# Joining a normalisation to a recurrence, and rotation tables to a projection, in a two-block model kernel

## The chip, the cores and the metric

The kernel runs on one core of a Trainium2 chip, as one program. The metric is the time of one execution on the device, in microseconds (us); of several executions the median counts. All arrays are float32. TensorE multiplies matrices, VectorE (DVE), ScalarE (ACT) and GpSimd (POOL) do elementwise work, and SyncE (SP) issues loads and stores.

## The reference

Two transformer-like blocks are computed over one sequence of 1024 tokens of width 1024. The parts that matter here are these.

In the first block eight heads of 64 run a recurrence over the tokens (`rwkv7_scan`). Its output y is normalised for each token and head, scaled and shifted for each channel, a bonus is added, and the sum is multiplied by a gate:

```python
y = rwkv7_scan(r_h, heads(decay), k_h, v_h, -kk, kk * a_h)
y = head_layernorm(y, LNX_EPS).reshape(Bn, T, C_R) * lnx_w + lnx_b   # mean and variance over the 64 of a head
bonus = jnp.sum(r_h * k_h * r_k, axis=-1, keepdims=True) * v_h
return ((y + bonus.reshape(Bn, T, C_R)) * g).astype(p.dtype)
```

In the second block eight attention heads have 128 plain and 64 rotated dimensions. The rotated part of the key, `k_pe`, is one of the outputs of the block's input projection and is shared by all heads:

```python
q = rmsnorm_2(q, qk_q_g)
k = rmsnorm_2(k, qk_k_g)                      # k = [k_nope, k_pe], mean of squares over 192
ang = positions.astype(jnp.float32)[..., None] * inv_freq
cos, sin = jnp.cos(ang)[:, :, None, :], jnp.sin(ang)[:, :, None, :]
q = concat(q[..., :128], apply_rope(q[..., 128:], cos, sin)); k = concat(k[..., :128], apply_rope(k[..., 128:], cos, sin))
```

## The kernel before

The program is a row of seventeen stages. Each is a block with a hand-written instruction order for every engine and semaphores between them. At the end of a stage its semaphores are cleared and all engines meet at a barrier. Stages hand their results on through scratch tensors in HBM. All tensors are laid out with channels on the 128 partitions and tokens along the free axis.

The order around the change is: `norm_dense_stage` "in1" (first input projection), `mlstm_stage`, `rwkv_scan_stage`, `rwkv_finish_stage`, the dense stages out1, up and down, `norm_stage`, `norm_dense_stage` "in2" (second input projection), the dense stages uq and ukv, `attention_stage`, and five more.

**The recurrence** (`rwkv_scan_stage`) handles 8 blocks b of 128 tokens, each of two chunks c of 64. It keeps three blocks of inputs loaded (`load(b)` on SP: `ar`, `bt`, `kt`, `vt`). For each block TensorE makes the products of the chunks (`first_products`), five groups of turned or multiplied inputs (`misc`), and a triangular inverse in five levels (`step_t`, `step_x`). Woven into the levels of block b are the three serial parts of block b-1 for each chunk: `z_part`, `u_part` and `s_part`. The last makes the change of the state, in PSUM bank `BANK_S`, and completes y, in `BANK_Y`. ScalarE copies PSUM to SBUF (`misc_copy`, `t_copy`, `z_copy`, `u_copy`, `y_copy`), VectorE masks the products (`first_masks`), merges levels (`level`) and updates the state (`state`), and GpSimd sets X and XT to the identity and masks two products. y of a block goes to HBM. After the loop the serial parts of the last block follow alone.

**The normalisation** (`rwkv_finish_stage`) is a stage of its own over four tiles of 128 channels by 1024 tokens: it loads y, the bonus and the gate, takes means and variances with matmuls, and ends with four VectorE passes for each tile. Its output goes to `cat`, which the dense stage out1 loads.

**The second input projection** runs over 37 tiles i of output channels. Each takes TensorE two halves of 512 tokens; VectorE copies each half out of PSUM (`acc` has four banks, so a half's bank is needed again two tiles later). The side work of `LruSide` runs between tiles: its last block n=7 uses the tiles i=29 to 32. GpSimd issues the stores, SP the weight loads.

**The attention** begins with loads of positions, `kpe` (tile 20 of the projection) and `kps` (the same with its rows swapped by halves of 64), then the first heads' q, k and v, all on SP. VectorE turns the positions into angles in eleven passes, ScalarE takes two sines, VectorE makes `cos_q`, `sin_q` and the rotated keys `krot` in six more. GpSimd squares q, k and the rotated parts; TensorE sums the squares over partitions (`sums`), ScalarE takes the root (`norms`), VectorE inverts (`inverses`) and scales the keys (`key_half`), and then the first `scores` can be made. From there 64 steps of head and query block run in a software pipeline.

## Time and profile before

| | us |
|---|---|
| median of three executions | 3876.27 |
| lowest, highest | 3863.0, 3878.07 |
| the profiled execution | 3871.72 |
| its span in the profile | 3870.2 |
| TensorE (matmul) busy in the span | 3233.1 |
| VectorE busy | 1597.6 |
| ScalarE busy | 945.3 |
| GpSimd busy | 509.8 |

The span runs from the first to the last instruction that the profile shows. Busy times are sums over all stages; engines overlap, so they don't add up to the span. In timelines a row gives start in us, length in us, engine, line, operation, output<-inputs, shapes and count; in brackets stands how long the engine was idle before it and what released it. "SPq" or "POOL ... DMA" is the issue of a transfer, not the transfer. One float32 matmul of TensorE is two records. L numbers are lines of the kernel.

### The profile page before, as it was taken

How to read it: one execution, taken by the hardware profiler on the slowest of the kernel's cores; microseconds unless marked ns; L12 is line 12 of the kernel's file. 1: busy time of each engine (PE TensorE's matmuls, PEld its weight loads, DVE VectorE, ACT ScalarE, POOL GpSimd, SP SyncE). 2: the span in 40 equal slices, each digit the busy share in tenths (PEclk: the TensorE clock that was granted, in tenths of full speed). 3: DMA queues.
4: the chain of work that ended last, by engine and by line, in shares of the span. 5: the costliest groups of instructions: out<-in, count | busy, mean ns of one | idle time of the engine just before them, and what ended most of it. 6: DMA issues, size and time to landing. Idle time of an engine off the chain costs nothing. (4 is left out here: it accounts for less than half of the span.)

```text
span 3870.2 us, 48977 instructions
## 1 busy us (share of the span) xinstructions
PE 3233.1 (84%) x20030; PEld 2376.7 (61%) x20030; DVE 1597.6 (41%) x2122; ACT 945.3 (24%) x1276; POOL 509.8 (13%) x539
## 2 busy tenths in 40 slices
PE   7997979967899997986899987598888884887774
PEld 6776339955688886774687766365676672322221
DVE  6664664433544444232644435666433312111112
ACT  5231442311211112121433321233322110111110
POOL 2211001100200000000200001634001002111111
PEclk9998789977899998998999998699999975899897
DMA  3322011124322223443322225311045461999996
GB/s 123 131 106 112 22 46 59 53 73 165 118 72 71 70 76 138 154 151 118 130 76 77 81 80 188 97 60 55 17 169 212 163 243 62 424 417 417 405 407 262
DMA packets 144443, 570.87 MB, mean 148 GB/s; under 512 B 21944, under 2 KB 46200, under 8 KB 123136
## 3 DMA queue, kind: packets, MB, share of 16 engines
q1 hardware_dynamic: 100384, 425.47, 29.3%
q0 software_dynamic: 42720, 130.15, 9.0%
q10 hardware_dynamic: 1152, 12.58, 0.8%
q8 instruction: 138, 2.26, 0.2%
q14 instruction: 49, 0.40, 0.0%
HBM read 463.17 MB, written 124.88 MB: 152 GB/s over the span
## 5 line engine op out<-in xcount | busy, mean ns | idle before, releaser
L52 PE MATMUL in_acc<-in_x_hi,in_w_hi 128*128 128x512 f32 x1024 | 411.8, 402 | 42.8 <-DVE in_x_lo L1536 38.9
L53 PE MATMUL in_acc<-in_x_lo,in_w_hi 128*128 128x512 f32 x1024 | 401.8, 392 | 0.0
L54 PE MATMUL in_acc<-in_x_hi,in_w_lo 128*128 128x512 f32 x1024 | 401.8, 392 | 0.0
L52 PE MATMUL up_acc<-up_x_hi,up_w_hi 128*128 128x512 f32 x704 | 276.4, 393 | 15.9 <-DVE up_x_lo L261 14.1
L53 PE MATMUL up_acc<-up_x_lo,up_w_hi 128*128 128x512 f32 x704 | 275.8, 392 | 0.0
L54 PE MATMUL up_acc<-up_x_hi,up_w_lo 128*128 128x512 f32 x704 | 275.8, 392 | 0.0
L52 PEld LDWEIGHTS in_acc<-in_x_hi,in_w_hi 128*128 128x128 f32 x1024 | 194.4, 190 | 93.6 <-issue 47.4
L2706 PE MATMUL ex_ap<-ex_wa,ex_xT 128*64 128x512 f32 x1088 | 242.2, 598 | 0.8 <-ACT ex_xT L2740 0.8
L53 PEld LDWEIGHTS in_acc<-in_x_lo,in_w_hi 128*128 128x128 f32 x1024 | 194.3, 190 | 44.3 <-issue 4.8
L54 PEld LDWEIGHTS in_acc<-in_x_hi,in_w_lo 128*128 128x128 f32 x1024 | 194.0, 189 | 41.2
L2706 PEld LDWEIGHTS ex_ap<-ex_wa,ex_xT 128*64 128x64 f32 x1088 | 78.0, 139 | 159.3 <-issue 158.1
L52 PE MATMUL down_acc<-down_x_hi,down_w_hi 128*128 128x512 f32 x352 | 141.1, 401 | 40.2 <-DVE down_x_lo L264 29.8
L2725 PE MATMUL ex_yp<-ex_wb,ex_hT 128*64 128x512 f32 x544 | 154.3, 719 | 22.2 <-ACT ex_hT L2751 22.2
L1470 ACT CAST in_w_hi<-in_w_raw 128x1024 fp32r<-128x1024 f32 x64 | 67.0, 1048 | 414.4 <-PE in_acc L54 389.0
L52 PEld LDWEIGHTS up_acc<-up_x_hi,up_w_hi 128*128 128x128 f32 x704 | 133.3, 189 | 44.9 <-issue 14.5
L54 PEld LDWEIGHTS up_acc<-up_x_hi,up_w_lo 128*128 128x128 f32 x704 | 133.3, 189 | 27.8
L53 PEld LDWEIGHTS up_acc<-up_x_lo,up_w_hi 128*128 128x128 f32 x704 | 133.4, 189 | 27.5
L2694 PE MATMUL ex_xp<-consts_sb,ex_xb 128*128 128x128 f32 x280 | 45.6, 315 | 124.7 <-DMA ex_xb<-s_u_tok,ex_idx 124.7
L53 PE MATMUL down_acc<-down_x_lo,down_w_hi 128*128 128x512 f32 x352 | 140.1, 398 | 0.0
L54 PE MATMUL down_acc<-down_x_hi,down_w_lo 128*128 128x512 f32 x352 | 139.8, 397 | 0.0
L1558 DVE TENSOR_TENSOR in_o_buf<-in_acc,in_rstd 128x512 f32<-128x512 f32 x68 | 46.8, 689 | 206.1 <-PE in_acc L54 205.8
L52 PE MATMUL out_acc<-out_x_hi,out_w_hi 128*128 128x512 f32 x256 | 101.7, 397 | 35.4 <-DVE out_x_lo L264 35.4
(539 smaller groups left out, 6145.7 us busy)
## 6 DMA issues: line engine op xcount, KB each, us to landing
ex_wa<-in_w SPq DMA_DIRECT2D x64, 2048.0 KB, 18.3
ex_wb<-in_ew SPq DMA_DIRECT2D x64, 1024.0 KB, 16.1
in_w_raw<-in_w_in SPq DMA_DIRECT2D x64, 512.0 KB, 3.7
up_w_raw<-in_w_up SPq DMA_DIRECT2D x44, 512.0 KB, 3.6
down_w_raw<-in_w_down SPq DMA_DIRECT2D x16, 1408.0 KB, 6.6
s_proj<-in_o_buf POOLq DMA_DIRECT2D x34, 512.0 KB, 2.9
s_ffn<-up_o_buf POOLq DMA_DIRECT2D x22, 512.0 KB, 3.1
down_x_raw<-s_ffn SPq DMA_DIRECT2D x44, 256.0 KB, 4.7
```

Source lines behind the costliest of these rows:

```text
L52: pe.matmul(out, w_hi, x_hi, start=first, stop=False)
L53: pe.matmul(out, w_hi, x_lo, start=False, stop=False)
L54: return pe.matmul(out, w_lo, x_hi, start=False, stop=last)
L1470: nc.scalar.copy(w_hi[:, j % 3, :], w_raw[:, j % 2, :]).then_inc(w_hi_done, 1)
L1558: nc.vector.tensor_tensor(dst[:, hs], acc[:, (i % 2) * NH + h, :], rstd[:, hs], ALU.mult).then_inc(acc_free, 1)
L2694: mm = pe.transpose(xp[:, k // 4, (k % 4) * P:(k % 4 + 1) * P], xb[:, q, k * P:(k + 1) * P], ident)
L2706: mm = pe.matmul(ap_[u * BS:(u + 1) * BS, :], xT[:, k * P + u * BS:k * P + (u + 1) * BS], wa[:, 2 * q + u, k * 512:(k + 1) * 512], start=k ...
L2725: mm = pe.matmul(yp[u * BS:(u + 1) * BS, n, :], hT[:, k * P + u * BS:k * P + (u + 1) * BS], wb[:, 2 * q + u, k * DM + n * 512:k * DM + (n ...
```

## The change

- `rwkv_finish_stage` is gone. The recurrence takes over its work, one block of 128 tokens at a time, while it works on later blocks. For block b-1 TensorE centres y with one 128x128 matmul over 512 columns into `BANK_S` (`center`, at level 4 of block b), ScalarE squares it, and TensorE takes the means of the squares into `BANK_Y` behind the last level (`variance`). In block b+1 ScalarE takes the root behind its first `misc_copy`; VectorE, behind `first_masks`, makes a reciprocal of 512 columns and two products (`scaled`); GpSimd adds the shift and the bonus and multiplies by the gate (`finish`), and SP stores to `cat`. `z_part` of the next block waits for the root, `s_part` for the first product. The bonus and the gate are loaded by blocks (`load_finish`). The masks tensor grows by 256 columns for the two matrices.
- First loads: masks, scale and block 0's `kt` and `vt` are issued on ScalarE, `ar` and `bt` of block 0 on SP. TensorE begins when `ar` and `bt` are there. SP waits for the first products before it loads the other blocks. In the loop SP stores block b before it loads block b+3.
- Angles, sines, `cos_q`, `sin_q` and `krot` are made in the second input projection, as side work: positions are loaded in `sync_first`, `kpe` and `kps` behind the last weights (`sync_last`), the VectorE passes run behind tiles 30 (`turns`), 33 (`angles`) and 35 (`rotations`), the sines behind tile 34. Three tiles go to a new scratch tensor `trig`.
- The attention loads `cos_q`, `sin_q`, `krot` and `kpe`. The four squares of head 0 are made by ScalarE, the two additions of 64 rows by VectorE. GpSimd waits for the four squares and then begins with head 0's gain and rotation. Later heads are as before.

The diff, cut to its core; `...` marks what is left out (the removed stage and the removed angle code among it):

```diff
-MASK_AFTER, MASK_IDENT, MASK_COLS = MASK_PAIR + 128, MASK_PAIR + 192, MASK_PAIR + 256
+MASK_AFTER, MASK_IDENT, MASK_COLS = MASK_PAIR + 128, MASK_PAIR + 192, MASK_PAIR + 512
+MASK_CENTER, MASK_MEAN = MASK_PAIR + 256, MASK_PAIR + 384
...
+    head = (np.arange(P)[:, None] // 64 == np.arange(P)[None, :] // 64) / 64.0
+    masks = np.concatenate(lv + below + [r < q, r <= q, r > q, r == q, np.eye(P) - head, head], 1).astype(np.float32)
...
+                sp.dma_start(bt[:, s, :, :, :].rearrange("p m c t -> p m (c t)"), cols(scr["bt"], 2 * CH, b)).then_inc(loaded[s], 16)
+                if b:
+                    for dst, name in ((kt, "kt"), (vt, "v")):
+                        sp.dma_start(dst[:, s, :, :, :].rearrange("p m c t -> p m (c t)"), cols(scr[name], 2 * CH, b)).then_inc(kv_loaded[s], 16)
+            def load_finish(b):
+                s = b % BUFS
+                if b >= BUFS:
+                    sp.wait_ge(yo_ready, b - BUFS + 1)
+                for dst, name in ((bon, "bonus"), (gate, "g")):
+                    sp.dma_start(dst[:, s, :, :, :].rearrange("p m c t -> p m (c t)"), cols(scr[name], 2 * CH, b)).then_inc(fin_loaded[s], 16)
             def store(b):
...
+                sp.wait_ge(yo_ready, b + 1)
+                sp.dma_start(cols(cat[0:4], 2 * CH, b), yo[:, :, :, :].rearrange("p m c t -> p m (c t)")).then_inc(stored[0], 16)
             load(0)
...
+            sp.wait_ge(ab_ready, 1)
+            for b in range(1, BUFS):
+                load(b)
+            for b in range(BUFS):
+                load_finish(b)
             for b in range(NB):
+                store(b)
                 if b + BUFS < NB:
                     load(b + BUFS)
-                store(b)
...
+            sp.wait_ge(stored[0], 16 * NB)
...
+                if b and c == 0:
+                    pe.wait_ge(rms_ready, b)
...
+                if b and c == 0:
+                    pe.wait_ge(yn_ready, b)
...
+            def center(b):
+                pe.wait_ge(y_copied, 2 * (b + 1))
+                pe.wait_ge(ds_done, 2 * (b + 1))
+                pe.matmul(ps[:, BANK_S, :], lv[:, MASK_CENTER:MASK_CENTER + P], ybuf[:, b % 2, :, :, :].rearrange("p m c t -> p (m c t)"),
+                          start=True, stop=True).then_inc(center_ready, 1)
+            def variance(b):
+                pe.wait_ge(sq_ready, b + 1)
+                pe.matmul(ps[:, BANK_Y, :], lv[:, MASK_MEAN:MASK_MEAN + P], sq[:, :, :, :].rearrange("p m c t -> p (m c t)"),
+                          start=True, stop=True).then_inc(var_ready, 1)
...
+                pe.wait_ge(kv_loaded[b % BUFS], 32 * (b // BUFS + 1))
...
+                        if b:
+                            center(b - 1)
...
+                if b:
+                    variance(b - 1)
...
+            center(NB - 1)
+            variance(NB - 1)
...
+            first = lambda t: t.rearrange("m p x -> p m x")[:, :, 0:2 * CH]
+            act.dma_start(lv[:, :], masks).then_inc(c_loaded, 16)
+            act.dma_start(scale[:, :, :], scr["scale"].rearrange("m p c -> p m c")).then_inc(c_loaded, 16)
+            act.dma_start(kt[:, 0, :, :, :].rearrange("p m c t -> p m (c t)"), first(scr["kt"])).then_inc(kv_loaded[0], 16)
+            act.dma_start(vt[:, 0, :, :, :].rearrange("p m c t -> p m (c t)"), first(scr["v"])).then_inc(kv_loaded[0], 16)
...
+            def squares(b):
+                act.wait_ge(center_ready, b + 1)
+                nc.scalar.activation(sq[:, :, :, :].rearrange("p m c t -> p (m c t)"), ps[:, BANK_S, :], ACT.Square).then_inc(sq_ready, 1)
+            def root(b):
+                act.wait_ge(var_ready, b + 1)
+                if b:
+                    act.wait_ge(inv_ready, b)
+                nc.scalar.activation(rms[:, :, :, :].rearrange("p m c t -> p (m c t)"), ps[:, BANK_Y, :], ACT.Sqrt,
+                                     bias=C[:, CONST["eps_ln"]:CONST["eps_ln"] + 1]).then_inc(rms_ready, 1)
...
+                if b >= 2:
+                    root(b - 2)
...
+                            squares(b - 1)
...
+            root(NB - 2)
...
+            squares(NB - 1)
+            root(NB - 1)
...
+            def scaled(b):
...
+                dve.wait_ge(rms_ready, b + 1)
+                if b:
+                    dve.wait_ge(yw_ready, b)
+                nc.vector.reciprocal(inv[:, :, :, :], rms[:, :, :, :]).then_inc(inv_ready, 1)
+                dve.wait_ge(inv_ready, b + 1)
+                tt(yn[:, :, :, :].rearrange("p m c t -> p (m c t)"), ps[:, BANK_S, :], inv[:, :, :, :].rearrange("p m c t -> p (m c t)"),
+                   ALU.mult).then_inc(yn_ready, 1)
+                dve.wait_ge(yn_ready, b + 1)
+                if b:
+                    dve.wait_ge(y1_ready, b)
+                tt(joined(yw[:, :, :, :]), joined(yn[:, :, :, :]), lnx, ALU.mult).then_inc(yw_ready, 1)
...
+                if b >= 2:
+                    scaled(b - 2)
...
+            scaled(NB - 2)
...
+            scaled(NB - 1)
...
+            def finish(b):
+                pool.wait_ge(yw_ready, b + 1)
+                nc.gpsimd.tensor_tensor(joined(y1[:, :, :, :]), joined(yw[:, :, :, :]), shift, ALU.add).then_inc(y1_ready, 1)
+                pool.wait_ge(y1_ready, b + 1)
+                pool.wait_ge(fin_loaded[b % BUFS], 32 * (b // BUFS + 1))
+                nc.gpsimd.tensor_tensor(y2[:, :, :, :], y1[:, :, :, :], bon[:, b % BUFS, :, :, :], ALU.add).then_inc(y2_ready, 1)
+                pool.wait_ge(y2_ready, b + 1)
+                if b:
+                    pool.wait_ge(stored[0], 16 * b)
+                nc.gpsimd.tensor_tensor(yo[:, :, :, :], y2[:, :, :, :], gate[:, b % BUFS, :, :, :], ALU.mult).then_inc(yo_ready, 1)
...
+                    finish(b - 2)
+            finish(NB - 2)
+            finish(NB - 1)
...
-def rwkv_finish_stage(nc, scr, y_out, V, C):
...
+            side.sync_last(sp, lambda n: sp.wait_ge(stored[n % 2], 16 * (n // 2 + 1)))
...
+        sp.dma_start(self.pos[:, :], self.positions.partition_broadcast(P)).then_inc(self.pos_loaded, 16)
+    def sync_last(self, sp, wait_stored):
+        wait_stored(self.kpe_at)
+        rows = self.proj[20]
+        sp.dma_start(self.kpe[:, :], rows).then_inc(self.kpe_loaded, 16)
+        for r in range(0, P, 64):
+            sp.dma_start(self.kps[r:r + 32, :], rows[r + 32:r + 64, :]).then_inc(self.kpe_loaded, 16)
+            sp.dma_start(self.kps[r + 32:r + 64, :], rows[r:r + 32, :]).then_inc(self.kpe_loaded, 16)
...
+        if i == 34:
+            act.wait_ge(self.ang_ready, 1)
+            self.nc.scalar.activation(self.xc[:, :], self.ang[:, :], ACT.Sin).then_inc(self.trig_ready, 1)
+            self.nc.scalar.activation(self.pre[:, 0:SEQ], self.cv[:, 1, :], ACT.Sin).then_inc(self.trig_ready, 1)
...
+        if i == 30:
+            self.turns(dve)
+        if i == 33:
+            self.angles(dve)
+        if i == 35:
+            self.rotations(dve)
...
+    def turns(self, dve):
...
+        dve.wait_ge(self.pos_loaded, 16)
+        dve.wait_ge(self.conv_ready, DT)
+        st.link(nc.vector.tensor_copy(t1, self.pos[:, :]))
+        st.link(ts(ang, t1, self.C[:, CONST["inv_freq"]:CONST["inv_freq"] + 1], None, ALU.mult))
...
+        st.link(ts(t1, t2, -self.MAGIC, None, ALU.add))
+    def angles(self, dve):
...
+        for c_ in (self.C1, self.C2, self.C3):
+            st.link(stt(out=ang, in0=t1, scalar=-c_, in1=ang, op0=ALU.mult, op1=ALU.add))
+        st.link(ts(ang, ang, 3.1415925, -3.1415925, ALU.min, ALU.max))
+        st.link(stt(out=t1, in0=ang, scalar=-1.0, in1=ang, op0=ALU.mult, op1=ALU.max))
+        ts(t2, t1, -1.0, self.TWO_PI / 4, ALU.mult, ALU.add).then_inc(self.ang_ready, 1)
+    def rotations(self, dve):
...
+        dve.wait_ge(self.trig_ready, 2)
+        st.link(ts(sin, sin, self.C[:, CONST["rope_sign"]:CONST["rope_sign"] + 1], None, ALU.mult))
+        dve.wait_ge(self.o_ready, DT)
+        tt(self.rg[:, :], cos, col("qg_r").to_broadcast([P, SEQ]), ALU.mult).then_inc(self.trig_done, 1)
+        tt(self.ig[:, :], sin, col("qg_s").to_broadcast([P, SEQ]), ALU.mult).then_inc(self.trig_done, 1)
+        dve.wait_ge(self.kpe_loaded, 80)
+        st(stt(out=t1, in0=self.kpe[:, :], scalar=col("kg_r"), in1=cos, op0=ALU.mult, op1=ALU.mult))
+        st(stt(out=t2, in0=self.kps[:, :], scalar=col("kg_s"), in1=sin, op0=ALU.mult, op1=ALU.mult))
+        st.settle()
+        tt(self.gel[:, :], t1, t2, ALU.add).then_inc(self.krot_done, 1)
     def pool(self, pool, i):
...
+        if i == 35:
+            pool.wait_ge(self.trig_done, 2)
+            pool.dma_start(self.trig[0], self.rg[:, :]).then_inc(self.trig_stored, 16)
+            pool.dma_start(self.trig[1], self.ig[:, :]).then_inc(self.trig_stored, 16)
+            pool.wait_ge(self.krot_done, 1)
+            pool.dma_start(self.trig[2], self.gel[:, :]).then_inc(self.trig_stored, 16)
...
+                    sp.dma_start(qr[:, :], qT[8 + h // 2]).then_inc(qr_loaded, 16)
+                    if h == 0:
+                        sp.dma_start(kpe[:, :], proj[20]).then_inc(kpe_loaded, 16)
+                        sp.dma_start(cos_q[:, :], trig[0]).then_inc(trig_loaded, 16)
+                        sp.dma_start(sin_q[:, :], trig[1]).then_inc(trig_loaded, 16)
                     for r in range(0, P, 64):
...
+                        sp.dma_start(qs[r:r + 32, :], qT[8 + h // 2][r + 32:r + 64, :]).then_inc(qs_loaded, 16)
+                        sp.dma_start(qs[r + 32:r + 64, :], qT[8 + h // 2][r:r + 32, :]).then_inc(qs_loaded, 16)
+                    if h == 0:
+                        sp.dma_start(krot[:, :], trig[2]).then_inc(krot_loaded, 16)
...
+            dve.wait_ge(first_sq, 4)
+            st(tt(q_sq[0:64, :], q_sq[0:64, :], qr_sq[0:64, :], ALU.add))
+            st(tt(k_sq[0:64, :], k_sq[0:64, :], kpe_sq[0:64, :], ALU.add))
             st.settle()
...
+            dve.sem_inc(sq_ready, 1)
+            dve.wait_ge(krot_loaded, 16)
...
+            act.wait_ge(h_loaded[0], 48)
+            nc.scalar.activation(q_sq[:, :], qn[:, 0, :], ACT.Square).then_inc(first_sq, 1)
+            nc.scalar.activation(k_sq[:, :], kn[:, 0, :], ACT.Square).then_inc(first_sq, 1)
+            act.wait_ge(qr_loaded, 16)
+            nc.scalar.activation(qr_sq[:, :], qr[:, :], ACT.Square).then_inc(first_sq, 1)
+            act.wait_ge(kpe_loaded, 16)
+            nc.scalar.activation(kpe_sq[:, :], kpe[:, :], ACT.Square).then_inc(first_sq, 1)
...
+            pool.wait_ge(first_sq, 4)
+            def squares(h):
...
+                        pool.wait_ge(trig_loaded, 32)
+                        pool.wait_ge(qr_loaded, 16)
+                    pool.wait_ge(qs_loaded, 64 * (h // 2 + 1))
```

## Rows read from the trace of the kernel before

**Rows 1.** The page, busy time of each engine: us, share of the span, instructions.

```profile
PE 3233.1 (84%) x20030; PEld 2376.7 (61%) x20030; DVE 1597.6 (41%) x2122; ACT 945.3 (24%) x1276; POOL 509.8 (13%) x539
```

**Rows 2.** Window, length, busy us of PE, PEld, DVE, ACT, POOL, then clock, DMA share, GB/s.

```profile
633.00:663.00 30.00, 29.59 (x929) 29.21 (x927) 13.28 (x32) 8.78 (x21) 4.02 (x6) 1.00 0.22 65
820.00:905.00 85.00, 33.78 (x112) 23.63 (x112) 26.24 (x28) 6.63 (x10) 3.06 (x6) 0.52 0.31 110
```

**Rows 3.** Timeline from the last y copy to the next dense stage's first load.

```profile
815.89 0.37 ACT L1112 COPY rs_ybuf<-rs_ps 128x256 f32<-128x256 f32 x1 [1.25 <-PE rs_ps L1040]
...
819.62 0.33 SPq L1239 DMA_DIRECT2D rf_y<-s_y  x1
...
832.93 1.28 ACT L1294 ACT_TABLE_LOAD   x1
...
900.99 0.81 SPq L136 DMA_DIRECT2D out_w_raw<-in_w_out  x2
```

**Rows 4.** Timeline of the mLSTM stage, passes of 512 columns.

```profile
547.05 1.13 PE L846 MATMUL ml_num<-ml_prod,ml_v_tok 128*128 128x512 f32 x2
...
561.50 0.69 DVE L741 SCALAR_TENSOR_TENSOR ml_v_sum<-ml_ss,ml_den_sq 128x512 f32<-128x512 f32 x1 [0.75 <-ACT ml_den_sq L794]
...
563.39 3.35 DVE L747 RECIPROCAL ml_inv<-ml_rms 128x512 f32<-128x512 f32 x1 [1.19 <-ACT ml_rms L800]
```

**Rows 5.** Timeline of the recurrence, start of its last block of tokens.

```profile
781.23 0.63 PE L1006 MATMUL rs_ps<-rs_tok,rs_mk 64*64 64x64 f32 x16
...
781.44 0.58 ACT L1094 COPY rs_raw<-rs_ps 128x512 f32<-128x512 f32 x1 [3.44 <-PE rs_ps L969]
...
782.11 1.27 POOL L1211 TENSOR_TENSOR rs_mk<-rs_raw,rs_lv 128x512 f32<-128x512 f32 x1 [4.85 <-ACT rs_raw L1094]
...
783.58 0.43 DVE L1164 COPY_PREDICATED rs_XT<-rs_lv,rs_mab 128x256 f32<-128x256 uint32 x1
...
786.30 0.63 PE L1032 MATMUL rs_ps<-rs_tok 64*64 64x64 f32 x16
```

**Rows 6.** DMA issues of the attention's start: tile, count, KB, median us to landing.

```profile
at_kpe<-s_proj SPq DMA_DIRECT2D x1, 512.0 KB, 5.5
```

**Rows 7.** Timeline behind the loop of the recurrence, z part and s part.

```profile
807.00 0.68 PE L1006 MATMUL rs_ps<-rs_tok,rs_mk 64*64 64x64 f32 x16 [0.31 <-ACT rs_tok L1094]
...
809.36 0.66 PE L1032 MATMUL rs_ps<-rs_tok 64*64 64x64 f32 x16
```

**Rows 8.** Timeline of the start of the recurrence.

```profile
571.97 0.38 SPq L923 DMA_DIRECT2D rs_ar<-s_ar  x1
...
578.45 0.48 PE L955 MATMUL rs_ps<-rs_bt,rs_ar 64*64 64x64 f32 x4 [17.18 <-DMA rs_vt<-s_v]
```

**Rows 9.** Timeline of VectorE at the end of the second input projection.

```profile
2280.01 0.69 DVE L1558 TENSOR_TENSOR in_o_buf<-in_acc,in_rstd 128x512 f32<-128x512 f32 x1 [4.68 <-PE in_acc L54]
...
2290.89 0.69 DVE L1558 TENSOR_TENSOR in_o_buf<-in_acc,in_rstd 128x512 f32<-128x512 f32 x1 [4.68 <-PE in_acc L54]
```

**Rows 10.** Timeline of the attention's start.

```profile
2415.45 0.34 SPq L2043 DMA_DIRECT2D at_pos<-in_positions  x1
...
2441.54 0.58 PE L2235 MATMUL at_pb<-consts_sb,at_q_sq 128*128 128x1 f32 x2 [31.01 <-POOLq L2330]
...
2446.84 1.06 ACT L2179 ACTIVATE at_sin<-at_ang 128x1024 f32<-128x1024 f32 x1 [30.11 <-DVE at_t L2094]
...
2447.96 0.57 PE L2235 MATMUL at_pb<-consts_sb,at_k_sq 128*128 128x1 f32 x2
...
2451.94 1.28 DVE L2101 SCALAR_TENSOR_TENSOR at_t<-at_kpe,vecs_sb,at_cos 128x1024 f32<-128x1024 f32 x1
...
2453.14 3.36 DVE L2102 SCALAR_TENSOR_TENSOR at_t<-at_kps,vecs_sb,at_sin 128x1024 f32<-128x1024 f32 x1
...
2459.81 0.25 DVE L2114 RECIPROCAL at_inv<-at_rms 128x16 f32<-128x16 f32 x1
...
2473.28 0.64 PE L2265 MATMUL at_score<-at_k_g,at_q_g 128*128 128x128 f32 x2
```

241 lines of the change are left out of this document (60 added, 181 removed).

## The prediction

> **What bounds the kernel now.** I read the page first. TensorE is busy for 84% of the span [rows 1], but that is a mean over seventeen stages that run one after the other, each closed by a barrier. So the change is read in the three places that it touches: the recurrence with the normalisation behind it, the end of the second input projection, and the start of the attention. The busy time by windows comes next. In the recurrence TensorE works 29.6 of 30 us at a granted clock of 1.00, so every matmul or wait put on it there costs its full length. In the 85 us of the normalisation stage it works 33.8 us at a clock of 0.52, VectorE 26.2, ScalarE 6.6: nothing is full, it is a chain of loads and steps [rows 2]. Last come the timelines, for who is released by whom.
>
> **Term 1, the normalisation stage goes.** Its first load is issued at 819.62, the first DMA of the next dense stage at 900.99: 81.4 us are removed, its loads, stores and barrier with them [rows 3]. From the end of the last y copy (816.26) to 819.62 there are 3.4 us, which are the store of y, its landing and the barrier; the new stage has the same after its last store, so they cancel.
>
> **Term 2, two matmuls for each block of 128 tokens.** The centring and the mean of squares are 128x128 matmuls over 512 columns. The nearest row is a pair of records, one float32 matmul of that size, in 1.13 us [rows 4]. Between them ScalarE squares the centred block (nearest: a copy of 512 columns, 0.58 [rows 5]), which is about hidden behind the 0.63 us group of matmuls issued between the two; I add 0.15 for hand-overs. 2 x 1.13 + 0.15 = 2.4 us, in seven blocks of the loop: +16.8. If the drain of a matmul overlaps the next it is 2 x 0.96 = 1.9; this is an estimate, so 13.4 is the lower end.
>
> **Term 3, the waits inside the loop.** TensorE's z part now waits for the root of the block before, since both use one PSUM bank, and ScalarE can only take that root after its first copy of the block. In the timeline z starts at 781.23; the copy runs from 781.44 to 782.02, the root (0.6) to 782.65, so z moves by 1.45 us. Everything of TensorE is queued behind it. VectorE finishes its first masks at 784.01 and then takes the new reciprocal of 512 columns, 3.35 us, and a multiply, 0.69 [rows 4]: ready at 788.1. The s part needs that (the bank with the centred block must be free); it stood at 786.30 [rows 5], now 787.75: 0.35 more. The second multiply (0.69) and the level copies behind it hold the next step for about 0.25. Together 2.05 us in six blocks: +12.3. Bounds: 0 if ScalarE gets its root in before, and, if nothing of VectorE's 4.75 us is hidden, 1.45 + 4.75 = 6.2 a block, 37.
>
> The three GpSimd passes of a finish, 1.27 us each by the nearest row [rows 5], fall in its idle time (4 us of work in a window of 30 [rows 2]). The first root needs an activation table, 1.28 us [rows 3]; behind the copy it is on the path: +1.3. The loads of later blocks now stand behind the store of a block finished two rounds later; they are then issued about half a block ahead of their use, against landings of 5.5 us [rows 6]: nothing.
>
> **Term 4, the tail.** After the loop z(7,0) waits for variance and root of the sixth block: the root, 0.7. The s part starts 2.36 after z [rows 7], while reciprocal and multiply take 4.15 from the root: +1.8. Then the last y copy, and a chain that has no cover at all: matmul 1.15, square 0.7, matmul 1.15, root 0.7, reciprocal 3.4, two multiplies 1.45, three GpSimd passes 4.05, so 12.6 us. Tail: +15.1.
>
> **Term 5, the first loads.** TensorE now starts on two tensors instead of four. Before, the first matmul came at 578.45, 6.5 us after the first issue, released by the fourth tensor [rows 8]. If the two first tensors stayed alone they would be there some 1.9 us sooner (768 of 1280 KB, taken as coming evenly over the last 4.7 us); but masks (now 655 KB), scale and the two other tensors are issued at the same time from ScalarE. I take -0.5, between -1.9 and +1.5. The Trainium skill ("DMA: Bandwidth & Descriptors", section "Issuing engines are not separate DMA queues") says that DMAs from several engines run on the same 16 DMA engines and interleave, and that spreading them saves only issue time. By that rule this term is near zero or slightly a loss, by the count of bytes alone -1.9; no run yet shows which.
>
> Recurrence and normalisation: -81.4 + 16.8 + 12.3 + 1.3 + 15.1 - 0.5 = **-36.4 us**.
>
> **Term 6, the end of the second input projection.** Eleven VectorE passes, two sines, one load of positions, five of rows and three stores move here. VectorE's last two waits there are for TensorE, which sets the pace at 10.9 us a tile [rows 9]. Six rotation passes of at most 1.28 us [rows 10] start at 2280.7, take 7.7, and with one half copy (0.69) are done before TensorE's last half at 2290.89. The angle passes lie one tile after another earlier, at most 7.7 us each, and the accumulator banks they hold back are wanted a tile later. Their loads and stores are issued while SP and GpSimd stand idle; behind the last GpSimd issue only this stage's own last store waits. The sine changes ScalarE's table, so the next stage reloads one, while it waits for TensorE. I take +0.5, between 0 and +4 (if the passes run slow).
>
> **Term 7, the start of the attention.** Before, 57.8 us pass from the first load (2415.45) to the first score (2473.28); VectorE's angle chain holds the inverse until 2459.81 [rows 10]. Without it the chain is: q, k, v landed about 7.2 us after the first issue (third in line, 5.5 us for a lone tile [rows 6], plus the sharing); four squares on ScalarE (nearest pass 1.06) until 11.4; two 64-row additions on VectorE; the sums on TensorE, 7.0 us (2441.54 to 2448.5) at the low clock; root 0.4; then 13.5 us from inverse to score as before. For the additions the trace has both prices of a pass with two SBUF inputs: 1.28 while GpSimd waits, 3.36 while GpSimd works [rows 10]. GpSimd is released by the same four squares, so it works: I take 5.5 for the two, between 2.5 and 6.7. The sum is 11.4 + 5.5 + 7.0 + 0.4 + 13.5 = 37.8: **-20 us**, between -14 (slower landings too) and -24. The Trainium skill ("GPSIMD Engine Reference", section "Key points") says that GpSimd shares its SBUF interfaces with VectorE and contends with instructions that have two SBUF inputs. With that rule the two additions cost about 6.7, without it 2.5; the two rows agree with the rule.
>
> The second queue past which work moves, GpSimd's, loses its five passes of squares here, but q times gain and the rotation start sooner (at 11.4 instead of 26) and end before the inverse.
>
> **Sum.** -36.4 + 0.5 - 20 = -56 us. The profiled execution took 3871.7 us (span 3870.2), so 3815.8; the median of the three runs is 4.6 above it, so by the median 3820.3. I say 3818. A change below 0.5% (19 us) can't be told from none in this kernel.
>
> **Rivals.**
> (A) As summed, 3818: 0.60.
> (B) The recurrence turns into a VectorE chain: no part of the reciprocal and the multiplies is hidden, 6.2 instead of 2.05 a block, +25 us: 3843. For it: 3.35 us is the longest single step there, and GpSimd's passes slow VectorE's. Against: VectorE works only 13.3 of 30 us, and TensorE has 5 us of queued work between z and s. 0.15.
> (C) The waits are hidden and the matmuls cost only 1.9: terms 2 and 3 are 13.4 instead of 29.1, the additions are undisturbed (-4): 3798. For it: TensorE's order could absorb it; against: it is in order and full. 0.12.
> (D) The attention's start gains only 8, because its loads land late (twelve of them now queued, the ones of 128 KB among them, with krot last) and the additions then hold the sums: 3830. Against: a lone tile of this size lands in 5.5 us [rows 6], and only q, k, v, qr and kpe are in front of the squares. 0.08.
> (E) Slower than before: the stalls of 1.5 to 2 us in each block, and the rows show a clock of 1.00 only with TensorE without gaps and 0.52 in the stage with gaps [rows 2], make the granted clock fall to 1.2 GHz in the loop. The eight blocks take some 29 us each (first matmul 578.45, last y copy 815.89 [rows 3, 8]); at half clock they would take twice that, so two of the eight eat the whole gain, and all eight would give +230, 4050. Against: it has still over 90% of its time busy. 0.05, of which 0.03 slower and 0.02 about even.
>
> **Range.** 3796 to 3843 holds A, C, D and most of B, and takes in the bounds of terms 2 to 7. Faster by over 0.5%: A, C, D, nearly all of B, 0.93; within 0.5%: 0.04; slower: 0.03.
>
> **What the profile will show.** The stage from its first load to the next stage's first DMA: before 329.0 us (571.97 to 900.99), after about 292.6. In a middle block, z starts about 1.5 us after the copy that it used to precede, and a block takes 4.4 us more than the some 29 of before. The two 512-column matmuls take about 1.1 each. The chain behind the last y copy is 12.6 to the store. In the attention 38 us from first load to first score, with the two additions at about 2.7 each. The second input projection as long as before, its last three stores behind nothing. It would be wrong if a block grows by over 7 us or under 2.5, if the clock in the loop is under 0.95, or if the last copy of the projection waits for VectorE.

## The result

The changed kernel takes 3821.85 us (median of four, 3819.11 to 3826.96) against 3871.36 us of the kernel before on the same chip (median of four, 3863.0 to 3878.07). The ratio is 0.9875, 95% interval 0.9849 to 0.9901: 1.25% faster. The profiled execution took 3819.11 us with a span of 3817.3, 52.9 less than before.

The page of the changed kernel: TensorE's busy time, and one of the DMA queues (packets, MB, share of the 16 engines' span), which is needed further down.

```profile
PE 3220.8 (84%) x19950; PEld 2360.4 (62%) x19950; DVE 1595.9 (42%) x2120; ACT 953.8 (25%) x1288; POOL 519.9 (14%) x556
...
q8 instruction: 138, 2.26, 0.2%
```

TensorE is busy for nearly as long as before [rows 1]; what went is time in which it stood. By the first and last issues of the stages the 52.9 us are: 1.0 before the recurrence, 30.8 in the recurrence and normalisation, 0.3 from there to the end of the second input projection, then a loss of 0.7 in the two dense stages behind it, 23.2 at the start of the attention, and a loss of 1.8 behind it.

**The loop.** By windows, one block of the loop and then the tail (columns as in [rows 2]):

```profile
740.00:775.00 35.00, 32.25 (x922) 29.64 (x920) 17.94 (x34) 9.97 (x23) 7.70 (x9) 1.00 0.22 64
845.00:870.00 25.00, 8.20 (x187) 6.05 (x183) 8.63 (x10) 3.14 (x7) 7.54 (x7) 0.77 0.07 22
```

TensorE has 32.3 us of work in 35 at a clock of 1.00, where it had 29.6 in 30 [rows 2]. The timeline from the middle of one block (the window 740 to 775) to the start of the next shows what lies between:

```profile
763.52 0.62 PE L1011 MATMUL rs_ps<-rs_T,rs_XT 64*64 64x64 f32 x15 [0.61 <-issue]
...
770.34 1.12 PE L1073 MATMUL rs_ps<-rs_ybuf,rs_lv 128*128 128x512 f32 x2
...
772.15 1.13 PE L1078 MATMUL rs_ps<-rs_sq,rs_lv 128*128 128x512 f32 x2
...
777.02 0.58 ACT L1143 COPY rs_raw<-rs_ps 128x512 f32<-128x512 f32 x1 [4.93 <-PE rs_ps L990]
777.51 0.69 ACT L1169 ACTIVATE rs_rms<-rs_ps,consts_sb 128x512 f32<-128x512 f32 x1
...
778.50 0.68 PE L1029 MATMUL rs_ps<-rs_tok,rs_mk 64*64 64x64 f32 x16 [1.52 <-ACT rs_raw L1143]
...
779.16 0.43 DVE L1229 COPY_PREDICATED rs_XT<-rs_lv,rs_mab 128x256 f32<-128x256 uint32 x1
...
779.80 3.35 DVE L1252 RECIPROCAL rs_inv<-rs_rms 128x512 f32<-128x512 f32 x1 [0.21 <-DVE rs_XT L1229]
...
783.19 0.69 DVE L1254 TENSOR_TENSOR rs_yn<-rs_ps,rs_inv 128x512 f32<-128x512 f32 x1
...
783.94 0.68 PE L1057 MATMUL rs_ps<-rs_tok 64*64 64x64 f32 x16
```

The two matmuls over 512 columns are there (770.34, 772.15), with the square between them. ScalarE makes the next block's first copy (777.02) and then the root (777.51), and only then z starts, after 1.52 us idle. VectorE ends its masks at 779.6, takes the reciprocal until 783.15 and the multiply, and the s part follows at 783.94. From one z part to the next (744.02 to 778.50) are 34.5 us, before 28.9. And there is a line for which the same block of the kernel before has no counterpart: 763.52, 0.61 us idle "<-issue", in the middle of the block, with nothing that the profile names as releaser.

**Start and tail.** The recurrence's first issue and first matmul (before: [rows 8]), and the steps behind the loop to the next dense stage's first DMA (before: [rows 3, 7]).

```profile
570.95 0.38 SPq L934 DMA_DIRECT2D rs_ar<-s_ar  x1
...
577.80 0.48 PE L976 MATMUL rs_ps<-rs_bt,rs_ar 64*64 64x64 f32 x4 [17.56 <-DMA rs_bt<-s_bt]
```

```profile
842.65 0.68 PE L1029 MATMUL rs_ps<-rs_tok,rs_mk 64*64 64x64 f32 x16 [0.93 <-issue]
...
846.61 0.68 PE L1057 MATMUL rs_ps<-rs_tok 64*64 64x64 f32 x16 [1.41 <-DVE rs_yn L1254]
...
852.95 0.37 ACT L1159 COPY rs_ybuf<-rs_ps 128x256 f32<-128x256 f32 x1 [1.25 <-PE rs_ps L1065]
...
864.51 1.26 POOL L1294 TENSOR_TENSOR rs_yo<-rs_y,rs_gate 128x512 f32<-128x512 f32 x1
869.15 0.82 SPq L136 DMA_DIRECT2D out_w_raw<-in_w_out  x2
```

The first matmul comes 6.85 us after the first issue (before 6.48). The stage ends at 869.15: 298.2 us from its first load, before 329.0.

**The end of the second input projection and the start of the attention.** VectorE's passes around the rotations (before: [rows 9]), then the attention's start (before: [rows 10]).

```profile
2248.41 0.75 DVE L2008 TENSOR_SCALAR in_xc<-in_xc,consts_sb 128x1024 f32<-128x1024 f32 x1
...
2255.13 0.68 DVE L1532 TENSOR_TENSOR in_o_buf<-in_acc,in_rstd 128x512 f32<-128x512 f32 x1
2258.68 0.69 DVE L1532 TENSOR_TENSOR in_o_buf<-in_acc,in_rstd 128x512 f32<-128x512 f32 x1 [2.87 <-PE in_acc L54]
```

```profile
2383.95 0.34 SPq L2096 DMA_DIRECT2D at_qn<-s_qT  x1
...
2391.20 1.06 ACT L2204 ACTIVATE at_q_sq<-at_qn 128x1024 f32<-128x1024 f32 x1 [17.62 <-DMA at_vt<-s_kvT]
...
2395.18 1.89 POOL L2367 TENSOR_TENSOR at_q_g<-at_qn,vecs_sb 128x1024 f32<-128x1024 f32 x1 [15.05 <-ACT at_kpe_sq L2209]
2395.20 2.94 DVE L2125 TENSOR_TENSOR at_q_sq<-at_q_sq,at_qr_sq 64x1024 f32<-64x1024 f32 x1 [8.98 <-ACT at_kpe_sq L2209]
2398.07 1.21 DVE L2126 TENSOR_TENSOR at_k_sq<-at_k_sq,at_kpe_sq 64x1024 f32<-64x1024 f32 x1
...
2407.08 0.22 DVE L2140 TENSOR_SCALAR at_neg_scale<-at_inv 128x8 f32<-128x8 f32 x1
...
2418.57 0.64 PE L2294 MATMUL at_score<-at_k_g,at_q_g 128*128 128x128 f32 x2
```

The six rotation passes run from 2248.41 to 2255.2; the last half copy still waits 2.87 us for TensorE. In the attention 34.6 us pass from first load to first score, before 57.8. This interval isn't always so short: in the eight other kernels that have the moved angles and the same code in the attention it was 34.4 and 34.6 in two and 35.8 to 38.0 in six (why, is said in the last section). So the gain lies between 20 and 23.5 us, and the changed kernel's profile shows one of the better cases.

### The profile page after: what moved, and what is told of

Same layout as the page of the kernel before. It is cut to its first block and busy times, and to the rows that moved or that the text cites. A ratio compares the mean times of both kernels' runs of the same rounds, so it can differ in the third digit from the quotient of the medians.

```text
span 3817.3 us, 48859 instructions
## 1 busy us (share of the span) xinstructions
PE 3220.8 (84%) x19950; PEld 2360.4 (62%) x19950; DVE 1595.9 (42%) x2120; ACT 953.8 (25%) x1288; POOL 519.9 (14%) x556
## 3 DMA queue, kind: packets, MB, share of 16 engines
q1 hardware_dynamic: 105952, 424.39, 29.6%
q8 instruction: 138, 2.26, 0.2%
## 5 line engine op out<-in xcount | busy, mean ns | idle before, releaser
L2729 PEld LDWEIGHTS ex_xp<-consts_sb,ex_xb 128*128 128x128 f32 x280 | 36.5, 162 | 159.3 <-DMA ex_xb<-s_u_tok,ex_idx 156.8
```

Source lines behind the costliest of these rows:

```text
L2729: mm = pe.transpose(xp[:, k // 4, (k % 4) * P:(k % 4 + 1) * P], xb[:, q, k * P:(k + 1) * P], ident)
```

## The experiments

All times are medians; the ratio is to the kernel before, measured beside it. "Stage" is from the recurrence's first load to the next dense stage's first DMA, "loop" from the first z part to the first one behind the loop, both in the profiled execution (whose own time lies up to 7.6 us from the median). For the kernel before they are 329.0 and 199.7.

| kernel | us | ratio (95%) | stage | loop |
|---|---|---|---|---|
| changed | 3821.85 | 0.9875 (0.9849 to 0.9901) | 298.2 | 235.8 |
| first part alone | 3841.67 | 0.993 (0.9912 to 0.9948) | 300.9 | 238.0 |
| second part alone | 3846.91 | 0.9943 (0.9925 to 0.9961) | | 199.3 |
| root earlier | 3821.48 | 0.9876 (0.9856 to 0.9897) | 301.4 | 237.9 |
| chain earlier | 3815.3 | 0.9863 (0.9842 to 0.9885) | 292.3 | 229.7 |
| loads spread | 3818.64 | 0.9868 (0.9852 to 0.9885) | 298.3 | 234.8 |
| chain and loads | 3807.04 | 0.9841 (0.9824 to 0.9857) | 288.1 | 224.7 |
| one queue | 3822.88 (one run) | | 301.2 | 239.6 |
| GpSimd later | 3824.34 (one run) | | 303.1 | 240.6 |
| table first | 3819.61 | 0.9871 (0.9856 to 0.9886) | 298.5 | 236.3 |
| best | 3795.47 | 0.9816 (0.9802 to 0.9829) | 278.1 | 218.6 |

Differences of up to 5 us in the last two columns are not the edit's unless a row shows where they are: "first part alone", "GpSimd later", "one queue" and "table first" have the changed kernel's loop, and it took 235.8 to 240.6 us in these five, of which the changed kernel's is the shortest. In "GpSimd later" the granted clock was 0.93 in the window 640 to 680.

### The two parts one by one

The first takes the changed recurrence into the kernel before and leaves projection and attention alone; the second does the reverse.

> The joined normalisation alone; the second input projection and the attention are those of the kernel before. The trace of the changed kernel gives 30.8 us for this part (329.0 to 298.2 from the first load of the recurrence to the next dense stage's first DMA). Theory: the two parts don't touch each other, so the time is 3871.4 - 30.8 = 3841, and the attention's start stays at 57.8 us. Rival: some of the gain of the attention came from the first part, or a stage between them changed; then the time is over 3846 or under 3836.

> The angles and rotated keys at the end of the second input projection alone; the recurrence and the normalisation stage are those of the kernel before. Theory: 57.8 to 34.65 us at the start of the attention, nothing in the projection: 3871.4 - 23.2 = 3848, and with the other part's 30.8 the two add up to the whole change within 3 us. Rival: the moved passes cost something in the projection that the other part hides; then the gain is under 20.

Measured: 28.4 us and 23.2 us under the kernel before (3870.08 beside them). Together 51.6, and the whole change 49.5. The parts add up within what the measurement can tell (each interval is some 7 us to either side), so a cost that one hides from the other is not excluded below that. In the profiles the attention's start took 59.1 us with the first part alone (expected 57.8) and 36.4 with the second (expected 34.65); the second part's expectation took the changed kernel's short interval for the rule.

### The root earlier

```diff
                 misc_copy(b, 0)
-                if b >= 2:
-                    root(b - 2)
...
                     if l < NL - 1:
                         t_copy(b, l + 1, 0)
+                if b:
+                    root(b - 1)
```

> Of the changed kernel only ScalarE's order is changed: the root of a block is taken right behind its squares, at the end of the block, instead of behind the first copy of the next block. TensorE then finds the bank free when it comes to z, so the wait of 1.5 us before z goes. Theory (two waits in a row, VectorE's is the real one): the masks end at the same time, the reciprocal and the multiply behind them end 4.1 us later as before, so the s part takes over what z gives back, its wait grows from 0.24 to about 1.8 us, and a block stays at 34.3 to 34.8 us: total within 3 us of the changed kernel. Rival (the prediction's split, 1.45 for z and 0.35 for s): the 1.5 us are won in each of six blocks, a block takes about 33.2 and the total falls by 9 us.

Measured: the same time. Timeline of a block's start:

```profile
779.65 0.63 PE L1029 MATMUL rs_ps<-rs_tok,rs_mk 64*64 64x64 f32 x16
...
782.00 0.43 DVE L1228 COPY_PREDICATED rs_XT<-rs_lv,rs_mab 128x256 f32<-128x256 uint32 x1
...
782.65 3.35 DVE L1251 RECIPROCAL rs_inv<-rs_rms 128x512 f32<-128x512 f32 x1 [0.21 <-DVE rs_XT L1228]
...
786.78 0.68 PE L1057 MATMUL rs_ps<-rs_tok 64*64 64x64 f32 x16 [1.90 <-DVE rs_yn L1253]
```

z now starts at 779.65 without the 1.5 us of waiting, and all of it comes back at the s part: 1.90 us idle, released by the multiply. VectorE's masks end as before 2.6 us behind the start of the block's first copy, and the reciprocal of 3.35 us stands behind them. So the z wait was not the price: it lay under a longer chain, VectorE's. Three blocks took 34.3 to 34.8 us as expected; 35.6 and 36.0 took the two in which the clock fell (one is shown below). The rival (33.2 us and 9 us less) falls.

This kernel shows one thing more. Behind the same wait in an earlier block (1.83 us) TensorE's groups of 16 matmuls, which start 0.47 us apart, start 0.85 us apart for a while; then the windows with the granted clock.

```profile
646.02 0.87 PE L1057 MATMUL rs_ps<-rs_tok 64*64 64x64 f32 x16 [1.83 <-DVE rs_yn L1253]
646.67 1.07 PE L1061 MATMUL rs_ps<-rs_us,rs_tok 64*64 64x64 f32 x16
647.52 1.07 PE L1065 MATMUL rs_ps<-rs_mab,rs_us 64*64 64x64 f32 x16
```

```profile
643.00:650.00 7.00, 5.17 (x124) 5.04 (x121) 5.94 (x7) 1.55 (x4) 4.34 (x4) 0.76 0.01 2
650.00:657.00 7.00, 7.00 (x242) 6.92 (x240) 2.16 (x6) 1.70 (x4) 0.57 (x1) 1.00 0.83 241
```

The granted clock of that stretch is 0.76, a mix of the levels of 2.4 and 1.2 GHz, after TensorE had stood for 1.83 us; in the next stretch it is 1.00 again. The five groups from 646.02 on come 1.5 us late in all.

### The chain earlier

```diff
+                if b >= 2:
+                    inverse(b - 2)      # the reciprocal
                 first_masks(b, 0)
                 first_masks(b, 1)
                 if b >= 2:
-                    scaled(b - 2)
+                    centred(b - 2)      # multiply with the bank
                 for l in range(NL):
...
                     level(b, l, 1)
+                    if l == 0 and b >= 2:
+                        weighted(b - 2)  # second multiply
```

> As the kernel with the early root, and VectorE takes the reciprocal ahead of the first masks of the next block, the multiply with the centred block behind the second masks, and the second multiply behind the first two level copies. Theory: of the 5.6 us that a block gained, 2.4 are the two matmuls and nearly all the rest is the chain root, masks, reciprocal, multiply; with the reciprocal (3.35) in VectorE's idle time it ends about 3.4 us sooner than s needs it, the masks of the first half come some 0.5 us late, so a block takes 31.5 to 32.5 us and the total falls by 12 to 19 us against the changed kernel: 3803 to 3810. Rival: the masks that wait for the reciprocal (2.5 us later) hold TensorE's first step as long as the reciprocal held the s part: a block over 34 us and nothing won.

Measured: 3815.3, 6 us less, half of what was expected. The intervals of the two ratios overlap, so the total alone doesn't show a gain; the loop does, with 229.7 us against 235.8 to 240.6 in the five executions of the changed loop. Timeline of VectorE's reciprocal at a block's start, and TensorE later in the same block:

```profile
769.47 3.35 DVE L1254 RECIPROCAL rs_inv<-rs_rms 128x512 f32<-128x512 f32 x1 [1.47 <-ACT rs_rms L1169]
...
775.14 0.54 PEld L1003 LDWEIGHTS rs_ps<-rs_X,rs_mab 64*64 64x64 f32 x16 [1.00 <-DVEq L1230]
...
796.42 0.45 PE L1011 MATMUL rs_ps<-rs_T,rs_XT 64*64 64x64 f32 x8 [1.29 <-issue]
```

The mechanism is as expected: the reciprocal lies in VectorE's idle time, the s part waits for nothing, and what is left is 0.87 us for masks that come late (775.14). From first copy to first copy three blocks took 32.8 to 33.1 us, where 31.5 to 32.5 were expected. The others took 34.0 and 35.5, and the windows of the last show why:

```profile
790.00:796.00 6.00, 5.13 (x172) 4.92 (x166) 2.39 (x6) 1.98 (x5) 0.74 (x2) 1.00 0.81 239
799.00:804.00 5.00, 4.92 (x60) 3.19 (x56) 0.44 (x1) 1.55 (x3) 0.75 (x2) 0.74 0.01 2
```

First a stretch with the DMA engines 0.81 busy and an idle piece of 1.29 us "<-issue", then one with a clock of 0.74. The rest of the gain was taken back by these; the changed kernel has such idle pieces too (0.61 in the timeline above), but no fall of the clock in its loop.

### The loads spread

In the changed kernel SP issues, in one go, the store of a finished block and six loads (first and last of the seven):

```profile
788.86 0.36 SPq L949 DMA_DIRECT2D s_cat<-rs_yo  x1
...
793.18 1.21 SPq L945 DMA_DIRECT2D rs_gate<-s_g  x1
```

```diff
             for b in range(NB):
-                store(b)
                 if b + BUFS < NB:
                     load(b + BUFS)
+                store(b)
+                if b + BUFS < NB:
                     load_finish(b + BUFS)
```

> Of the changed kernel only the order of SP's queue is changed: the four loads of a later block are issued ahead of the store of a finished block, as soon as their buffer is free (two thirds through a block), and only the store and the two loads of the finish stay at their place (a third through a block). So seven DMAs in a row become four and three. Theory: the idle pieces of TensorE in the middle of a block that wait for nothing the profile shows (0.36, 0.31, 0.78 with 0.16, 0.61 and 0.66 us in blocks 2 to 6, each a few us behind such a burst, with the DMA engines over 0.8 busy) are its instructions coming late behind the burst; they shrink below 0.4 and the total falls by 1 to 4 us against the changed kernel. Rival: they have nothing to do with the loads and stay at 0.3 to 0.8; same time.

> The kernel with the early chain and the spread loads. In the early chain alone a block took 32.8 to 33.1 us and two took 34.0 and 35.5: idle pieces of 1.41 and 1.29 us without a releaser, and behind the second a granted clock of 0.78 for 8 us. Theory: without the burst these go, every block takes 32.0 to 32.6 (28.9 + 2.4 for two matmuls + 0.87 for the masks that come late), and the total is 4 to 7 us below that of the early chain alone, near 3809. Rival: the pieces are not the loads' doing, blocks stay at 33 to 35 and the time at 3815.

Measured: in the changed kernel the pieces were 0.36, 0.31, 0.78 with 0.16, 0.61 and 0.66 us; with the loads spread one of 0.78 is left, and the last two full blocks take 33.7 instead of 34.4 and 34.7. In total 3818.64 against 3821.85, which alone can't be told from no change. With the early chain as well, a single piece of 0.84 is left behind the first z part and the clock is 1.00 throughout; the block with that piece takes 33.5 us and the four others 32.48 or 32.49 each, 28.9 + 2.4 + 0.87 and 0.3 more. The total of 3807.04 is what was expected, and 8 us below the early chain alone, though the intervals of the two ratios overlap.

All traces together decide between the theory and the rival, better than these two. The idle pieces of 0.3 us and more "<-issue" between the first z part and the last block's end (the wait with the table left out) sum to 2.7 to 4.9 us in the seven kernels with seven DMAs in a row (the changed one has the 2.7, the first part alone the 4.9, with a piece of 1.69), and to 0.55 to 0.84 us in the three with four and three; the kernel before has 0.32. In the loop's first block, ahead of all this, a piece of up to 1.4 us stands in kernels of both orders.

What the page calls the instruction queue (q8: 138 packets, 2.26 MB, so 16 KB each) is DMA like any other, and three such packets fall into 715 to 730 us, as in the kernel before. The Trainium skill ("Runtime: NRT & Kernel Launch", section "Instruction fetch mechanics") says that an engine's instructions are fetched in such blocks through a DMA queue of its own, and that this is mostly hidden. In the kernel before nothing in the loop speaks against that (one piece of 0.32 us "<-issue"); behind a burst of seven DMAs TensorE stands. That these packets wait behind the burst is argued from the place and from what spreading did; no row shows one packet waiting.

### The first loads on one queue

Masks, scale, kt and v of block 0 go from ScalarE's queue back to SP's, in the order ar, bt, kt, v, masks, scale.

> Of the changed kernel only the first loads of the recurrence are put back on SP's queue: the four tensors of block 0, then masks and scale, nothing from ScalarE. Read in the profile, not in the total. In the changed kernel the first matmul starts 6.85 us after the first issue, before the change 6.48. Theory (all DMAs share the same engines, so a second queue only brings the masks in between): the two tensors that TensorE waits for land in 5.5 to 6.5 us, that is the first matmul comes 0.3 to 1.3 us sooner than with two queues, and the masks land later, so that VectorE's first mask comes later. Rival (the prediction's bound by bytes): two queues bring the first tensors sooner; here the first matmul comes 7 us or more after the first issue.

```profile
571.94 0.38 SPq L934 DMA_DIRECT2D rs_ar<-s_ar  x1
...
576.18 0.48 PE L978 MATMUL rs_ps<-rs_bt,rs_ar 64*64 64x64 f32 x4 [14.96 <-DMA rs_bt<-s_bt]
...
581.20 0.69 DVE L1222 TENSOR_TENSOR rs_mab<-rs_ps,rs_lv 128x512 f32<-128x512 f32 x1 [8.86 <-DMA rs_scale<-s_scale]
```

The first matmul comes 4.24 us after the first issue, against 6.85 with two queues (6.5 to 7.2 in all eight kernels that have them, and 4.4 in the last kernel below, which has one). That is sooner than the theory's 5.5 to 6.5, and the rival falls. The masks land later: GpSimd, whose first copy needs them, starts 9.2 us after the first issue instead of 7.1. VectorE's first pass, which the theory had later, comes at 9.26 instead of 9.83, since it had waited longer for the matmuls. The first copy of the second block stands 35.3 us after the first issue, against 36.1 with two queues (35.8 to 37.2 in the eight) and 35.5 before the change (35.9 in the second part alone, which keeps that order). So two queues cost about 0.8 us against before by the means, and the 0.2 that one queue gains is within the scatter. The total, a single run, says nothing on that.

### GpSimd later in the attention

```diff
-            pool.wait_ge(first_sq, 4)
+            pool.wait_ge(sq_ready, 1)
```

> Of the changed kernel only GpSimd's first wait in the attention is changed: it starts its first pass behind VectorE's two additions instead of beside them. Read at the start of the attention. Theory (contention of passes with two SBUF inputs): the first addition falls from 2.94 to about 1.21 us, the sums start 1.7 us sooner, and the first score comes at 32.9 instead of 34.65 us after the first load; GpSimd's rotation ends later but still ahead of the first score. Rival: GpSimd's passes now run 1.8 us later beside VectorE's small passes behind the inverse, where one of 8 elements took 1.90 instead of 0.22 us before the change, and eat the gain: 34.5.

```profile
2389.13 0.34 SPq L2096 DMA_DIRECT2D at_qn<-s_qT  x1
...
2395.82 1.06 ACT L2204 ACTIVATE at_q_sq<-at_qn 128x1024 f32<-128x1024 f32 x1 [17.05 <-DMA at_vt<-s_kvT]
...
2399.82 1.22 DVE L2125 TENSOR_TENSOR at_q_sq<-at_q_sq,at_qr_sq 64x1024 f32<-64x1024 f32 x1 [8.42 <-ACT at_kpe_sq L2209]
...
2409.98 1.65 DVE L2140 TENSOR_SCALAR at_neg_scale<-at_inv 128x8 f32<-128x8 f32 x1
...
2422.91 0.64 PE L2294 MATMUL at_score<-at_k_g,at_q_g 128*128 128x128 f32 x2
```

Both mechanisms are there, and the price is nearly the rival's. The first addition takes 1.22 instead of 2.94 us. But GpSimd's rotation now lies over VectorE's scale of 8 elements behind the inverse, and that takes 1.65 instead of 0.22. The first score comes after 33.8 us, 0.8 less, of which 0.6 are loads that landed sooner: 1.7 won at the addition, 1.4 lost at the scale. One execution can't tell the edit from the phase of GpSimd's passes, which moves the same interval by up to 3 us in the other kernels.

### The table first

One square root of a 128x1 constant as ScalarE's first instruction of the stage.

> The changed kernel with one square root of a 128x1 constant added as ScalarE's first instruction of the recurrence, so that the table is loaded while it waits for the first copy. Theory: the table load (1.28 us) ahead of the first root goes from the path of the second block's z, whose wait falls from 2.84 to about 1.43 us; total 1.3 us lower, and the granted clock has no fall behind that wait (three of the other kernels had one there: 0.96 in the stretch 640 to 680, a period of 36.0 instead of 34.9 us). Rival: the copies in between bring back another table, the load stays at the first root and nothing changes.

Measured: the only table load of the stage now lies in ScalarE's idle time, the wait of the second block's z fell from 2.84 to 1.43 us, with a clock of 1.00 behind it. The period that ends with it is 33.0 us instead of 34.4. The same wait of 2.84 us was followed by a fallen clock in three kernels (loads spread and one queue 0.96, GpSimd later 0.93 in the window 640 to 680), and in two it was not (changed, first part alone). The ratio of 0.9871 against 0.9875 is too small a step to be told from none.

### All together

```diff
                     step_x(b, l, 0)
+                    if l == 4 and b:
+                        center(b - 1)
                     step_t(b, l, 1)
...
                         misc(b, 4)
                         if b:
-                            center(b - 1)
+                            variance(b - 1)
```

This with ScalarE's squares moved accordingly, the early chain, the spread loads, one queue, the table first, and the last block's three GpSimd passes on VectorE.

> The early chain with the spread loads, and four things more: the centring matmul of a block one step earlier, ahead of the step that waits 0.41 us for VectorE, with the mean of squares where the centring was; the first loads on SP's queue alone; the table loaded at the start; and the last block's three GpSimd passes on VectorE. Theory: a block falls from 32.48 to 31.3 to 31.7 us (the wait of 0.41 is covered, root and reciprocal come 0.8 us sooner, so the 0.87 for the masks go), six blocks give 5 to 7 us; the start gives 0.7, the table nothing more, the waits of 0.93 and 1.41 in the tail up to 2, the last passes 1.5. Total 3807 - 10 = 3797, between 3794 and 3801. Rival: the centring waits for the copy of y or the state, and moves TensorE's wait instead of removing it: blocks stay at 32.5 and the total at 3803.

```profile
755.46 1.13 PE L1077 MATMUL rs_ps<-rs_ybuf,rs_lv 128*128 128x512 f32 x2
...
760.19 3.35 DVE L1254 RECIPROCAL rs_inv<-rs_rms 128x512 f32<-128x512 f32 x1
...
766.08 0.54 PEld L1007 LDWEIGHTS rs_ps<-rs_X,rs_mab 64*64 64x64 f32 x16 [1.00 <-DVEq L1230]
```

Measured: 3795.47 us, 1.84% under the kernel before; its interval lies wholly below that of the changed kernel, and by the ratios of the medians it is 23 us faster. From the kernel with chain and loads alone the intervals don't quite separate it; the loop does (218.6 against 224.7 us). The last four periods of the loop take 31.71 or 31.72 us each, the upper end of what was expected: the wait of 0.41 us is covered by the centring (755.46) and the mean of squares comes earlier, as expected. The 0.86 us for the masks stayed (766.08), against the expectation: the reciprocal starts at 760.19, behind the root and a level copy that itself waits for TensorE's last step, so it didn't move with the mean of squares as far as it should. The three last passes take 0.69 each and the chain behind the last y copy is 1.6 us shorter. The two waits in the tail were to give up to 2 us and gave 0.4 (0.32 and 1.64 instead of 0.93 and 1.41). Four edits more than in the kernel with chain and loads stand together here, so only what a row shows is put down to one of them.

## Why the prediction was right, and where not

The time (3821.85, forecast 3818), the side and the case (A) came out. The nearness of the time is in part luck: 3818 was a gain of 58 us from a median of 3876.27, and measured were 49.5 from one of 3871.36 (52.9 in the profiled executions, forecast 56). In the recurrence 5.6 us of the gain stayed out, and the attention gave 3.2 more than forecast, about half of it by where GpSimd's passes happened to lie, which is not the same in other kernels with this code. None of the signs of being wrong is there: a block grew by 5.4 us on average, the clock in the loop was 1.00, the projection's last copy waits for TensorE. By its terms:

**Term 1, stage removed.** From the tail's z part to the next stage's first DMA 26.5 us pass, before 94.0 [rows 3, 7]: -67.5, where terms 1 and 4 without the root's 0.7 gave -67.0 (-81.4 + 15.1 - 0.7). The 3.4 us behind the last pass are there too (865.77 to 869.15).

**Term 2, two matmuls a block.** 1.05 and 1.06 us until the next group can start, and 0.29 until the squares are there: 2.4, as said.

**Term 3, waits.** The step "together 2.05 us in six blocks" was nearly right in its sum (z 1.5, s 0.3, level 0.2) and wrong in what makes it: taking away the z wait alone gave nothing, since masks, reciprocal and multiply set the start of the s part. It was rival B's chain that decided, at the price of A, because 5 us of TensorE's work lie between z and s. The mis-sized term is the whole block: 5.6 us more from z to z instead of 4.45, of which 0.8 is the idle piece "<-issue" with what is around it, that no term had, and the rest small pieces in the issue of the groups behind a wait. From the loop's second block to the tail's z part that is 36.0 us against 31.1 forecast, 4.9 of the 5.6 us by which the stage missed (-30.8 instead of -36.4). Of these 4.9 us the idle pieces make 2.9 by their rows. The other 2 us or so are of the kind that stays in a block without a piece: with the loads spread such a block takes 33.7 us, 4.85 more than before where 4.45 were forecast. The step that failed is "the loads of later blocks ...: nothing": it asked when they land, not what else stops while they are under way. The table load was as said (2.84 against 1.43 us).

**Term 4, tail.** Root wait 0.9 (0.7 forecast), s part later by 1.6 (3.96 from z to s against 2.36 before; forecast 1.8), last chain 12.45 from the end of the y copy to the last pass (12.6).

**Term 5, first loads.** -0.5 forecast, +0.6 measured at the first copy of the second block (+0.8 by the means of the kernels with this start), inside the bounds. With the same six DMAs in one row the first two land 2.6 us sooner. This agrees with the rule of the Trainium skill ("DMA: Bandwidth & Descriptors", section "Issuing engines are not separate DMA queues") that the queues share the same DMA engines; the bound by bytes alone, -1.9, would have needed the first two tensors to have them for themselves.

**Term 6.** No cost: six passes of 6.8 us instead of 7.7, the last half copy waits for TensorE. From the end of the recurrence to the end of this projection 0.3 us less pass than before.

**Term 7, attention.** -23.2 instead of -20, inside its bounds. Squares from 7.25 to 11.1 us (7.2 and 11.4 forecast), additions 2.94 + 1.21 = 4.15 instead of 5.5 (the forecast of 2.7 each was wrong for both): GpSimd's first pass is over before the second addition starts, since its next one waits for a load. Sums 7.0 as said. From inverse to score 11.8 instead of 13.5: the scale of 8 elements took 0.22 us here and 1.90 before. This last was not forecast and is luck: with the same code it is 13.3 to 15.1 us in six of eight other kernels.

The rivals: C fell (the waits aren't hidden), D fell (the loads of the squares landed after 7.25 us, and nothing waits for krot), E did not happen in the changed kernel's profile (clock 1.00 in the loop) but is real in small: falls of a few us behind a wait or an idle piece in five of the other kernels, two of them with the same loop; the one counted cost 1.5 us, far from what E would need.

## What to carry to other kernels

When a step is put into a loop of the full engine, look for the latest of the chains that meet at a wait, and move the start of that one: taking away the wait in front gives nothing. Long passes of a helper engine (a reciprocal of 512 columns) go where that engine is idle, even ahead of work that seems more urgent. And transfers that are issued in one burst may cost something though each lands in time: spread them over the loop's period. Last, a single profile of an edit can mislead by some us: the same loop took 235.8 to 240.6 us in five kernels, the same start of the attention 34.4 to 38.0 in nine.

## What the runs showed of the hardware

- A VectorE pass can be held by GpSimd whatever its own size: the scale of 128x8 elements behind the inverse took 0.17 to 0.36 us in four kernels and 1.4 to 1.9 us in eight, the one before among them (in one of the eight the scale next to it took this time). Its code is the same in all. It is short where it falls between two GpSimd passes or at the end of one, and where it is long it ends when GpSimd's pass does. The pass of 1024 columns behind it, with two SBUF inputs, shows the same: 1.2 us in six kernels, 2.8 to 2.9 in the other six, as here in "chain earlier":

```profile
2404.35 2.87 DVE L2155 TENSOR_TENSOR at_diag<-consts_sb,at_inv 128x1024 f32<-128x1024 f32 x1
```

  From inverse to score this makes 11.8 to 11.9 us where both passes are short (three kernels), 13.2 to 13.5 with one long (four), 14.5 to 15.1 with both (five): 3 us of the attention's start are a matter of phase. The Trainium skill ("GPSIMD Engine Reference", section "1. Specifications") names contention for VectorE instructions with two SBUF inputs or in a two-port mode; that a pass of 8 elements pays it in full is these traces' number.
- Seven DMAs in a row were followed by idle pieces of TensorE of 0.3 to 1.7 us with no releaser, 2.7 to 4.9 us in all in each of seven kernels; in groups of four and three 0.55 to 0.84 us were left.
- A wait or idle piece of TensorE of 1.3 to 2.8 us between stretches of full work was followed by a few us at a lower granted clock in some executions (behind 1.29, 1.83, 1.90 and 2.84 us) and not in others with the same wait (1.90 and 2.84 us).
- Six DMAs from one queue delivered the first two tensors within 4.2 and 4.4 us (two kernels), from two queues within 6.5 to 7.2 (eight).
